# Weight tiles read column by column from two halves in turn

## The reference, cut to what matters

```
proj = rms_norm(x) @ w_in          # 2048 -> about 5700 columns, then attention, compression
x    = x + mix @ w_out             # 2048 -> 2048
h    = rms_norm(x)
x    = x + (silu(h @ w_gate) * (h @ w_up)) @ w_down      # width 5632 between
# the second block the same way, with a convolution and attention as the mixer,
# and scales, shifts and gates from c @ ada_w
```

## Time and profile before

| | us |
|---|---|
| median of 3 runs | 2215.75 (2215.17 to 2216.69) |
| span of the profiled execution, first to last instruction | 2213.5 |
| TensorE busy in it | 2190.3 |
| VectorE busy | 1602.6 |
| ScalarE busy | 1097.1 |
| GpSimd busy | 236.2 |

### The profile page before, as it was taken

One profiled execution on the slowest core, in us unless ns is written; L12 is line 12 of the kernel. 1 busy time (PEld: TensorE's weight loads), 2 busy tenths in 40 slices (PEclk: granted clock), 3 DMA queues, 4 the chain that ended last, 5 costly groups with the idle time before them and its releaser, 6 DMA issues.

```text
span 2213.5 us, 29238 instructions
## 1 busy us (share of the span) xinstructions
PE 2190.3 (99%) x9949; PEld 1812.7 (82%) x9949; DVE 1602.6 (72%) x2077; ACT 1097.1 (50%) x1537; POOL 236.2 (11%) x215
## 2 busy tenths in 40 slices
PE   9999999999999999999999999999999999999998
PEld 7888888888888888888888887788888888888886
DVE  7656688888787878778866898897887455554555
ACT  6555574544434444344455776654444444434444
POOL 5004000000000000000002886000010000000000
PEclk9999999999999999999999999999999999999999
DMA  8776629899988998899746674768997677766764
GB/s 284 210 211 190 196 73 326 270 298 299 295 291 288 301 307 286 293 290 306 266 146 202 191 212 145 270 227 257 305 299 245 194 201 203 204 191 191 201 203 146
DMA packets 376233, 526.46 MB, mean 238 GB/s; under 512 B 120856, under 2 KB 129432, under 8 KB 375856
## 3 DMA queue, kind: packets, MB, share of 16 engines
q1 hardware_dynamic: 375536, 523.87, 76.0%
q10 hardware_dynamic: 576, 1.05, 0.2%
HBM read 510.15 MB, written 2.10 MB: 231 GB/s over the span
## 4 chain that ended last, share of the span: by engine, by line
PE 92%; DVE 3%; ACT 2%; DMA 1%; issue 1%; POOL 1%; SPq 0%; DVEq 0%; ACTq 0%; POOLq 0%
PE bank L1181 31%; PE bank L1197 29%; PE bank L1198 29%; DVE w_both L2250 1%; DMA raw<-in_w_in 1%; POOL convT L969 1%; PE bank L1252 1%; PE bank L1285 0%; PE bank L1273 0%; PE bank L1320 0%; ACT w_both L1671 0%; ACT zsb L1612 0%; DMA x_t<-in_x_t 0%; PE bank L1071 0%; PE bank L1166 0%
## 5 line engine op out<-in xcount | busy, mean ns | idle before, releaser
L2250 DVE TENSOR_TENSOR w_both<-raw,w_both 128x1024 fp32r<-128x1024 f32 x762 | 945.9, 1246 | 508.5 <-ACT w_both L1671 499.5
L1671 ACT ACTIVATE w_both<-raw 128x1024 fp32r<-128x1024 f32 x762 | 805.5, 1060 | 991.0 <-PE bank L1181 914.0
L1197 PE MATMUL bank<-w_both,act_hi 128*128 128x512 f32 x1984 | 774.2, 390 | 0.0
L1198 PE MATMUL bank<-w_both,act_lo 128*128 128x512 f32 x1984 | 772.2, 389 | 0.0
L1181 PE MATMUL bank<-w_both,act_hi 128*128 128x512 f32 x2160 | 576.1, 390 | 0.8 <-issue 0.5
L1181 PEld LDWEIGHTS bank<-w_both,act_hi 128*128 128x128 f32 x2160 | 404.1, 188 | 86.1 <-DVE w_both L2250 1.5
L1197 PEld LDWEIGHTS bank<-w_both,act_hi 128*128 128x128 f32 x1984 | 372.5, 188 | 76.8 <-issue 0.2
L1198 PEld LDWEIGHTS bank<-w_both,act_lo 128*128 128x128 f32 x1984 | 372.5, 188 | 76.6
L1197 PE MATMUL bank<-w_both,mid_hi 128*128 128x512 f32 x960 | 376.0, 392 | 3.9 <-DVE mid_lo L2382 2.4
L1198 PE MATMUL bank<-w_both,mid_lo 128*128 128x512 f32 x960 | 373.7, 389 | 0.0
L2208 DVE SCALAR_TENSOR_TENSOR ada_acc<-ada_raw,c_act,ada_acc 128x512 f32<-128x512 f32 x360 | 269.8, 749 | 11.5 <-DMA ada_raw<-in_ada_w 4.4
(11 more groups left out here) (319 smaller groups left out, 1010.6 us busy)
## 6 DMA issues: line engine op xcount, KB each, us to landing
ada_raw<-in_ada_w SPq DMA_DIRECT2D x192, 512.0 KB, 5.4
raw<-in_w_gate SPq DMA_DIRECT2D x176, 512.0 KB, 4.6
raw<-in_w_up SPq DMA_DIRECT2D x176, 512.0 KB, 4.9
raw<-in_w_down SPq DMA_DIRECT2D x176, 512.0 KB, 4.5
raw<-in_w_in SPq DMA_DIRECT2D x166, 512.0 KB, 4.4
raw<-in_w_out SPq DMA_DIRECT2D x60, 512.0 KB, 5.4
h_tok<-h_blk SPq DMA_DIRECT2D x256, 32.0 KB, 4.3
x_res<-in_x SPq DMA_DIRECT2D x8, 256.0 KB, 5.7
```

Of the source, the lines that this page charges most:

```text
L1197: pe.matmul(A_[t][:, :], h_, w_hi[:, s, kk, :], start=(k == 0), stop=False)
L1198: pe.matmul(A_[t][:, :], l_, w_hi[:, s, kk, :], start=False, stop=False)
L1671: act.activation(w_hi[:, U % SPLIT_SLOTS].rearrange("p k n -> p (k n)"), raw_of(c, u).rearrange("p k n -> p (k n)"), ACT.Copy).then_inc(hi ...
L2250: dve.tensor_tensor(w_lo[:, U % SPLIT_SLOTS].rearrange("p k n -> p (k n)"), raw_of(c, u).rearrange("p k n -> p (k n)"), w_hi[:, U % SPLIT_ ...
```

## The change

Four helpers build access patterns. `in_turn` reads a 512-column tile as column 0 of its first half, column 0 of its second half, column 1 of the first, and so on; `pairs` gives the PSUM bank the same shape without changing its order. `apart` reads a raw tile in its order, as pairs; `by_half` walks `w_hi` or `w_lo` so that the first of each pair goes to the first half and the second to the second half, 256 numbers further. So the even columns of a weight tile now lie in its first half and the odd ones in its second, and the matmul puts them in order again. All products use it but those of the compression.

```diff
@@ -618,6 +618,22 @@
 
         block = top.enter_context(nc.Block())
 
+        def in_turn(tile):
+
+            return tile.rearrange("p (a b) -> p b a", a=2)
+
+        def pairs(bank_):
+
+            return bank_[:, :].rearrange("p (b a) -> p b a", a=2)
+
+        def apart(tile):
+
+            return tile.rearrange("p k (b a) -> p k b a", a=2)
+
+        def by_half(tile):
+
+            return tile.rearrange("p k (a b) -> p k b a", a=2)
+
         def full_of(kind):
 
             return (cost_mid, prob_mid)[kind][:, :, :].rearrange("p a n -> p (a n)")[:, 0:NSA_G * T]
@@ -1030,7 +1046,7 @@
                         else:
                             pe.wait_ge(lo_done, u + 1)
                         for t in range(TT):
-                            ins = pe.matmul(A_[t][:, :], a[:, k, t * P:(t + 1) * P], w[:, u, kk, :],
+                            ins = pe.matmul(pairs(A_[t]), a[:, k, t * P:(t + 1) * P], in_turn(w[:, u, kk, :]),
                                             start=(k == 0 and a is act_hi and w is w_hi), stop=False)
                     if kk == KPU - 1:
                         ins.then_inc(parts_used, 1)
@@ -1178,7 +1194,7 @@
                     for kk in range(KPU):
                         k = KPU * u + kk
                         for t in tiles:
-                            ins = pe.matmul(A_[t][:, :], a[:, k, t * P:(t + 1) * P], w[:, s, kk, :],
+                            ins = pe.matmul(pairs(A_[t]), a[:, k, t * P:(t + 1) * P], in_turn(w[:, s, kk, :]),
                                             start=(k == 0 and a is hi and w is w_hi),
                                             stop=(stop and k == KPU * nu - 1))
                     return ins
@@ -1194,8 +1210,8 @@
                     k = KPU * u + kk
                     for t in tiles:
                         h_, l_ = hi[:, k, t * P:(t + 1) * P], lo[:, k, t * P:(t + 1) * P]
-                        pe.matmul(A_[t][:, :], h_, w_hi[:, s, kk, :], start=(k == 0), stop=False)
-                        pe.matmul(A_[t][:, :], l_, w_hi[:, s, kk, :], start=False, stop=False)
+                        pe.matmul(pairs(A_[t]), h_, in_turn(w_hi[:, s, kk, :]), start=(k == 0), stop=False)
+                        pe.matmul(pairs(A_[t]), l_, in_turn(w_hi[:, s, kk, :]), start=False, stop=False)
                 pe.wait_ge(lo_done, at(U + 1, r, 2 * nu))
                 return part(hi, w_lo, stop=True)
 
@@ -1492,7 +1508,7 @@
                     ins = act.activation(act_hi[:, k, :], x_t[:, k, :], ACT.Copy, scale=norm_scale[:, 0, k:k + 1])
                     ins.then_inc(half_hi if kk == 0 else act_hi_done, 1)
                     act.wait_ge(raw_half[u] if kk == 0 else raw_loaded[u], 16)
-                    ins = act.activation(w_hi[:, u, kk, :], raw[:, u, kk, :], ACT.Copy)
+                    ins = act.activation(by_half(w_hi[:, u, kk:kk + 1, :]), apart(raw[:, u, kk:kk + 1, :]), ACT.Copy)
                     ins.then_inc(half_hi if kk == 0 else hi_done, 1)
 
             def tile_hi(i):
@@ -1668,8 +1684,11 @@
                         act.wait_ge(raw_loaded[R % RAW_SLOTS], at(16 * (R // RAW_SLOTS + 1), r, 16 * 2 * c["nu"] // 4))
                     if U >= SPLIT_SLOTS:
                         act.wait_ge(parts_used, at(U - SPLIT_SLOTS + 1, r, 2 * c["nu"]))
-                    act.activation(w_hi[:, U % SPLIT_SLOTS].rearrange("p k n -> p (k n)"),
-                                   raw_of(c, u).rearrange("p k n -> p (k n)"), ACT.Copy).then_inc(hi_done, 1)
+                    if c["C"] is None:
+                        act.activation(w_hi[:, U % SPLIT_SLOTS].rearrange("p k n -> p (k n)"),
+                                       raw_of(c, u).rearrange("p k n -> p (k n)"), ACT.Copy).then_inc(hi_done, 1)
+                    else:
+                        act.activation(by_half(w_hi[:, U % SPLIT_SLOTS]), apart(raw_of(c, u)), ACT.Copy).then_inc(hi_done, 1)
                     after(u)
                     if c["C"] in KEPT_IN and u == (2 if KEPT_IN[c["C"]][0] == "plain" else 3):
                         post(KEPT_IN[c["C"]], None, None)
@@ -1938,7 +1957,8 @@
                         dve.wait_ge(half_hi, 2 * u + 2)
                     else:
                         dve.wait_ge(hi_done, u + 1)
-                    dve.tensor_tensor(w_lo[:, u, kk, :], raw[:, u, kk, :], w_hi[:, u, kk, :].bitcast(F32),
+                    dve.tensor_tensor(by_half(w_lo[:, u, kk:kk + 1, :]), apart(raw[:, u, kk:kk + 1, :]),
+                                      by_half(w_hi[:, u, kk:kk + 1, :].bitcast(F32)),
                                       ALU.subtract).then_inc(half_lo if kk == 0 else lo_done, 1)
 
             def tile_lo(i):
@@ -2247,10 +2267,14 @@
                     dve.wait_ge(hi_done, at(U + 1, r, 2 * nu))
                     if U >= SPLIT_SLOTS:
                         dve.wait_ge(parts_used, at(U - SPLIT_SLOTS + 1, r, 2 * nu))
-                    dve.tensor_tensor(w_lo[:, U % SPLIT_SLOTS].rearrange("p k n -> p (k n)"),
-                                      raw_of(c, u).rearrange("p k n -> p (k n)"),
-                                      w_hi[:, U % SPLIT_SLOTS].bitcast(F32).rearrange("p k n -> p (k n)"),
-                                      ALU.subtract).then_inc(lo_done, 1)
+                    if c["C"] is None:
+                        dve.tensor_tensor(w_lo[:, U % SPLIT_SLOTS].rearrange("p k n -> p (k n)"),
+                                          raw_of(c, u).rearrange("p k n -> p (k n)"),
+                                          w_hi[:, U % SPLIT_SLOTS].bitcast(F32).rearrange("p k n -> p (k n)"),
+                                          ALU.subtract).then_inc(lo_done, 1)
+                    else:
+                        dve.tensor_tensor(by_half(w_lo[:, U % SPLIT_SLOTS]), apart(raw_of(c, u)),
+                                          by_half(w_hi[:, U % SPLIT_SLOTS].bitcast(F32)), ALU.subtract).then_inc(lo_done, 1)
                     after(u)
                     if c["C"] in KEPT_IN and u == (2 if KEPT_IN[c["C"]][0] == "plain" else 3):
                         post(KEPT_IN[c["C"]], None, None)
```

## The result

| | before | after |
|---|---|---|
| median us (lowest to highest) | 2215.67 (2215.17 to 2216.69) | 2409.74 (2407.32 to 2411.62) |
| span of the profiled execution, us | 2213.5 | 2405.4 |
| mean granted clock | 0.999 | 0.977 |

The kernel became slower by 194 us, ratio 1.0875 (1.086 to 1.089). In the kernel after, the products stand at lines 1197, 1213 and 1214 (1181, 1197 and 1198 before), ScalarE's split at 1691, VectorE's at 2276.

A forecast was written before the change was run, and what follows sets the result against it. The prediction took TensorE's 9,120 matmuls to bound the kernel. It summed 2213.5 + 6,077 (matmuls) + 2 (exposed half splits) = 8,293 us of span, said as 8,300 us, range 4,000 to 8,600.

The forecast's parts named there:

- (1): The 9,120 matmuls reading scattered columns: 893 ns each instead of 0.2267 us, +6,077 us.
- Step (2): VectorE's 762 subtractions, scattered access: +0.72 us each, 1.97 us a split, some +549 us of work, hidden under TensorE.
- the sum: Whole kernel: 2213.5 + 6,077 + 2 = 8,293 us of span, given as 8,300 us.
- (3): ScalarE's 762 copies writing scattered: at most about 2 us each, hidden; half splits of the first two units expose 1 to 3 us.
- the sign: Direction of the whole kernel's time: slower, with chance 0.89.
- Step (4): DMA transfers: same bytes, raw slots freed later and wanted later by TensorE, costing nothing.
- TensorE doesn't notice, VectorE takes over: Rival: TensorE's step stays 0.2267 us, subtractions 0.72 to 1.44 us longer bind; 2,300 to 2,700 us, chance 0.09.
- It gets faster: Rival: alternating addresses remove TensorE's lost cycle, no split grows much; -122 us, 2,094 us, chance 0.08.
- The two that built on a price per column for TensorE: Rivals: two clock periods per column, 4,040 to 4,280 us, chance 0.20; surcharge added, 587 ns a matmul, 5,500 us, 0.10.
- the forecast (0.50): Likeliest case for TensorE's products: 893 to 907 ns a matmul, 8,300 us in all, chance 0.50.

The follow-up runs named there:

- the distance and hop rows: Matmul patterns timed outside the kernel, two places read in turn: hop of four columns within eight 0.2165 us a product, distance of 512 columns 0.216 us.
- half after half: Against the changed kernel, same layout, but splits read raw with a step of two and read and write w_hi and w_lo in order: 2175.7 us, ratio 0.9825 to before.

## Why the prediction was wrong

**The step that failed** is (1): "a scattered column needs a whole fetch", 893 ns a matmul. It measured 215.8, so the term of +6,077 us was in truth -99 by the step and -89 in the kernel's time. The price came from line 2491 (1.75 ns an element), taken as that of reads which lie apart. But that row walks eight places in turn and line 1973 steps by 64 bytes; the change walks two. With eight in turn TensorE too is slow, 0.490 us, and even that is a little over half of the 893. TensorE's price, as the rows read, goes with how many blocks of four numbers it reads in turn and how much of each it uses: all of two blocks in turn, 0.216; of four, 0.28; of eight, 0.49; one number of each block, 0.43 to 0.46; two numbers of each, 0.45 in one stream but 0.227 in two streams in turn. One rule that gives all of these I don't have. The match of TensorE's 4 x 0.443 = 1.77 ns with VectorE's 1.745 was a coincidence. The prediction named what would undo it, a port "that keeps two lines open, so that each is hit four times"; the distance and hop rows fit that, as a reading of the steps; how the port does it no run shows, and runs of two (0.339) don't follow from it, nor does a step of two in one stream.

The Trainium skill ("Advanced Engine Details and Errata", Memory Cachelines) wants two hits on a 16-byte line and has another line at each access cost. The traces agree for a step of four (0.4615 us for 512 columns on TensorE), for VectorE's reads with a step of two (1225 ns, as in order) and for TensorE's two streams with a step of two (0.227, as in order). They differ at two points: a step of two in one stream hits each line twice and still costs TensorE 0.451, and two lines visited in turn, another at each access, cost TensorE nothing and VectorE's reads 15 ns in 1024 elements (ScalarE's do pay, 227 ns). From the Trainium skill ("TensorE: Matmul & The Clock Gate", Back-to-back issue gap) comes an estimate of 215.8 ns for 512 columns; the reads in turn and bf16 show 215.8, contiguous ones here 226.7. For this kernel that rule was the better forecast of TensorE's step.

**Step (2)** had +0.72 us for the subtraction; it measured +0.945. By itself the pattern costs 0.83, of which the scattered write makes 0.71 and the scattered read beside it 0.12 (0.015 without the write): the size was near, but the working took it from reads. That it fits under the 10.7 us of a unit fell with step (1): the unit is 2.59 us, and 2.19 with an adaLN step of two 0.75 us is 3.7. So what the sum had as hidden, with (3), cost 283 us, and that alone made the kernel slower: the sign was right by luck, for the term that carried it had the other sign. **Step (3)** bounded the copy at 2.0 us; 2.18 was outside by a little (1.97 by itself). It was not hidden entirely either: 41 us with VectorE's splits in order. **Step (4)**, the transfers at nothing, held as far as any run bears on it: the splits took the same beside transfers as without. The compression's products, untouched, took 278 ns each at line 1336, where the earlier trace rows have 277.

**The rivals.** What happened is two of them at once. "TensorE doesn't notice, VectorE takes over" (chance 0.09) is the kernel with the splits alone: between its 2,300 at +0.72 and 2,700 at +1.44, the measured +0.98 gives 2,444, and 2,447 was measured. Its working by stretches came out right in the total; only its chance was small. "It gets faster" (0.08) is the kernel with the products alone: 0.2158 instead of its 0.2133 makes 99 us and not 122, and 2,126 was measured. Its condition, a split that grows by less than 0.36 us, fits only roughly: at +0.29 (half after half) less than half of the gain was left, at 0 nearly all. The two that built on a price per column for TensorE, with 0.30 between them, fell with the forecast. These two and the forecast (0.50) drew on one assumption, that a scattered column costs TensorE more than one in order, so their 0.80 was really one chance.

## What to carry to other kernels

A price read from one engine's access pattern holds for that pattern only: count how many blocks are walked in turn and how many of a block's numbers are used before it is left, look at reads and writes apart, and measure the very pattern, since the same two numbers of each block cost TensorE 0.451 or 0.227 by the order of the blocks. Where a rearranged layout is wanted, let it be written in runs of two or more, or let the reader of the result sort it; here both kept the whole gain of 4% that single writes had turned into a loss of 9%. And when several forecasts share one assumption, their chances fall together: the range should reach to what is left without it.

## What was unexpected of the hardware

- Contiguous fp32r columns are not the fastest: 0.2267 us for 512, in turn from two places 0.216. Why the former are slower is open.
- Runs of two from two places (0.339) cost more than single ones (0.216) or runs of four (0.251), and a step of two costs 0.451 in one stream, 0.227 in two. Open.
- GpSimd, whose instructions nobody touched, slowed as VectorE's subtraction grew longer, whatever made it long. The addition to `convT`, 128x256, took 1116 ns before (subtraction 1246), 1090 with ScalarE's copies alone scattered (1231), 1161 with products alone (1256), 1300 half after half, where nothing is written scattered (1539), 1535 with VectorE's splits alone as in the change (2120) and 1587 in the change (2191). That GpSimd waits for VectorE's instructions would fit; no run shows it. The reduction over partitions (`ada_row`) took 4186 ns before, 4397 half after half and 8990 with VectorE's splits as in the change. In the kernel after, each of the two stands for 2% of the chain that ended last. The first row is of the kernel with subtractions in order, the second of the one with copies in order (groups on GpSimd):

```profile
L985 POOL TENSOR_TENSOR convT<-convT,ada_raw 128x256 f32<-128x256 f32 x120 | 129.0, 1090 | 29.8 <-ACT ada_raw L1673 26.7
```
```profile
L985 POOL TENSOR_TENSOR convT<-convT,ada_raw 128x256 f32<-128x256 f32 x120 | 180.7, 1535 | 4.3
```

- Even-odd reads of VectorE and ScalarE go from 1.25 to 1.55 us and from 1.15 to 1.60 only beside TensorE reading in turn, not beside TensorE reading in order or beside transfers.
